# Mixer weights split once and loaded in parts by later blocks; layernorms' wide passes on VectorE

## The reference

```python
h = layernorm(concat([meta, x]), ln0_g, ln0_b)
proj = h @ w_in                       # q, k, v, conv B, C, h, and two gates
y_attn = window_attention(q, k, v, sinks) @ w_attn_out
y_conv = (cb * causal_conv3(cc * ch)) @ w_conv_out
mix = (sigmoid(ga) * y_attn + sigmoid(gc) * y_conv) @ w_o
h = layernorm(alpha * h + mix, ln1_g, ln1_b)
# then a router, top 2 of 32 experts, and a last layernorm
```

## Time and profile before

| | us |
|---|---|
| median of 3 runs | 4335.98 (4330.54 to 4336.49) |
| the profiled execution | 4333.28 |
| its span, first to last instruction | 4331.5 |
| first product of strip 0 in block 0, from the span's start | 62.7 |
| end of the last strip | 2690.2 |

### The profile page before, as it was taken

The page is one execution under the profiler, slowest core; times in us unless marked ns, Lnnn a source line. Parts: engine busy times, 40 slices in busy tenths (PEclk is TensorE's granted clock), DMA queues, the critical chain, the costliest instruction groups (busy, mean ns, idle before and its releaser), DMA issues. The chain is left out here.

```text
span 4331.5 us, 62892 instructions
## 1 busy us (share of the span) xinstructions
PE 4171.0 (96%) x20252; PEld 3428.8 (79%) x20253; DVE 2518.7 (58%) x3263; ACT 1773.0 (41%) x2950; POOL 1094.6 (25%) x1117
## 2 busy tenths in 40 slices
PE   7999999999999999999999999499999999999997
PEld 7887887887887888888888887388788888778886
DVE  5555555555555655645645645777666666765664
ACT  2422422422422422422422422466555555654553
POOL 4022032022022021121121121134333333333333
PEclk9999999999999999999999999799999999999998
DMA  6333333333333333333332332187666666765562
GB/s 171 85 107 103 93 102 98 99 104 97 102 104 89 107 106 85 107 104 89 111 102 80 117 102 78 54 289 248 246 199 198 206 199 234 251 203 198 194 204 90
DMA packets 569472, 601.49 MB, mean 139 GB/s; under 512 B 104080, under 2 KB 426640, under 8 KB 569248
## 3 DMA queue, kind: packets, MB, share of 16 engines
q1 hardware_dynamic: 521152, 476.88, 35.5%
q0 software_dynamic: 48096, 121.71, 8.4%
HBM read 527.15 MB, written 124.78 MB: 151 GB/s over the span
## 5 line engine op out<-in xcount | busy, mean ns | idle before, releaser
L826 PE MATMUL bank<-hT_hi,w_hi 128*128 128x512 f32 x2176 | 864.8, 397 | 30.1 <-DVE w_lo L658 21.3
L658 DVE TENSOR_TENSOR w_lo<-raw,w_hi 128x1024 fp32r<-128x1024 f32 x400 | 597.3, 1493 | 485.5 <-ACT w_hi L517 484.4
L827 PE MATMUL bank<-hT_lo,w_hi 128*128 128x512 f32 x2176 | 850.6, 391 | 2.4 <-issue 2.4
L828 PE MATMUL bank<-hT_hi,w_lo 128*128 128x512 f32 x2176 | 849.2, 390 | 0.0
L1565 PE MATMUL e_bank<-e_w_hi,e_xT_hi 128*128 128x512 f32 x1312 | 521.9, 398 | 14.2 <-DVE e_xT_lo L1488 12.4
L826 PEld LDWEIGHTS bank<-hT_hi,w_hi 128*128 128x128 f32 x2176 | 408.9, 188 | 140.4 <-DVE w_lo L658 32.6
L1567 PE MATMUL e_bank<-e_w_hi,e_xT_lo 128*128 128x512 f32 x1312 | 514.3, 392 | 0.0
L1566 PE MATMUL e_bank<-e_w_lo,e_xT_hi 128*128 128x512 f32 x1312 | 513.4, 391 | 0.0
L1493 DVE TENSOR_TENSOR e_w_lo<-e_raw,e_w_hi 128x1024 fp32r<-128x1024 f32 x384 | 444.4, 1219 | 117.7 <-ACT e_w_hi L1441 110.8
L828 PEld LDWEIGHTS bank<-hT_hi,w_lo 128*128 128x128 f32 x2176 | 408.9, 188 | 87.4
L827 PEld LDWEIGHTS bank<-hT_lo,w_hi 128*128 128x128 f32 x2176 | 409.3, 188 | 86.6 <-issue 5.4
(11 more groups left out here) (277 smaller groups left out, 7173.3 us busy)
## 6 DMA issues: line engine op xcount, KB each, us to landing
raw<-in_w_in_dram SPq DMA_DIRECT2D x251, 512.0 KB, 3.9
e_raw<-in_w_exp_gate_dram SPq DMA_DIRECT2D x128, 512.0 KB
e_raw<-in_w_exp_up_dram SPq DMA_DIRECT2D x128, 512.0 KB
e_raw<-in_w_exp_down_dram SPq DMA_DIRECT2D x128, 512.0 KB
h_rows<-h_rows SPq DMA_DIRECT2D x72, 512.0 KB, 3.5
raw<-in_w_o_dram SPq DMA_DIRECT2D x64, 512.0 KB, 3.8
raw<-in_w_in_dram SPq DMA_DIRECT2D x64, 256.0 KB, 3.7
raw<-in_w_attn_out_dram SPq DMA_DIRECT2D x64, 256.0 KB, 2.8
```

The source lines that it names most:

```text
L658: v.tensor_tensor(w_lo[:, s % 2, :], raw[:, s % RAW, :], w_hi[:, s % 2, :].bitcast(FP32), ALU.subtract).then_inc(lo_ready, 1)
L826: pe.matmul(out, hi, x_hi, start=first, stop=False)
L827: pe.matmul(out, hi, x_lo, start=False, stop=False)
L828: return pe.matmul(out, lo, x_hi, start=False, stop=last)
```

## The change

- In block 0 the weights are split as before, but two strips ahead, from 3 raw buffers, into three of four slots that each hold both parts of a strip; SP stores each split strip (1 MB) in DRAM, in `split_weights`.
- In blocks 1 to 7 no weights are split. SP loads both parts of strip s+3 from `split_weights` (1 MB, 8 KB per partition) into a slot, after strip s is done.
- The first block is written out ahead of a loop over the other seven.
- The layernorms of the loop do both wide passes on VectorE; GpSimd keeps the deviations.
- An `out` strip's first multiply waits for the last `mixT_lo`.

```diff
-    RAW = 5
+    RAW, META_RAW = 3, 5
+    SLOTS = 4
+    ahead = RAW
+    slot_of = list(range(SLOTS)) * 5 + [0, 1, 2] + list(range(SLOTS)) * 6 + [0, 1, 2]
+    def first_slot(s):
+        return (s + 1) % RAW
...
             def _(sp):
-                def load(s, b):
-                    hold(sp, lo_ready, b * N + s + 1)
-                    for dst, src in strip_dmas(*strips[s % N], raw[:, s % RAW, :]):
+                def load_raw(s):
+                    if s >= RAW:
+                        sp.wait_ge(lo_ready, s - RAW + 1)
+                    for dst, src in strip_dmas(*strips[s], raw[:, s % RAW, :]):
                         sp.dma_start(dst, src).then_inc(raw_in[s % RAW], 16)
-                load(0, 0)
-                with sp.Fori(0, BLOCKS) as b:
+                def store_split(s):
+                    sp.wait_ge(lo_ready, s + 1)
+                    sp.dma_start(split_d[s], slots[first_slot(s)][:, :, :].rearrange("p h d -> p (h d)").bitcast(FP32))\
+                      .then_inc(w_out[first_slot(s)], 16)
+                def load_split(s, b):
+                    sp.wait_ge(w_out[first_slot(s)], 16 * (sum(first_slot(q) == first_slot(s) for q in range(s + 1))))
+                    sp.dma_start(slots[slot_of[s]][:, :, :].rearrange("p h d -> p (h d)").bitcast(FP32), split_d[s])\
+                      .then_inc(w_in[slot_of[s]], 16)
+                def block_of_loads(b, first):
                     for s in range(N):
-                        load(s + 1, b)
+                        if first:
+                            store_split(s)
+                        if first and s + ahead < N:
+                            load_raw(s + ahead)
+                        else:
+                            hold(sp, strip_done, b * N + s + 3)
+                            if first:
+                                sp.wait_ge(w_out[first_slot(s)],
+                                           16 * (sum(first_slot(q) == first_slot(s) for q in range(s + 1))))
+                            load_split((s + ahead) % N, b + (s + ahead) // N)
                         if s - 3 in LN1_AT:
...
                         if s in X_AT:
...
@@ gpsimd
-                def scale(n, i1, rows, gain, shift):
-                    po.wait_ge(ln_normed, n + 1)
-                    po.tensor_tensor(rows[:, i1, :], rows[:, i1, :], gain[:, :], ALU.mult).then_inc(ln_scaled, 1)
-                    po.wait_ge(ln_scaled, n + 1)
-                    po.tensor_tensor(rows[:, i1, :], rows[:, i1, :], shift[:, :], ALU.add).then_inc(ln_done, 1)
...
@@ scalar, split_hi: in block 0 alone
+                        if first and s + 2 < N:
+                            split_hi(s + 2)
...
@@ vector
                 def normalize(n, i1, rows):
                     v.wait_ge(ln_moments, n + 1)
                     v.wait_ge(ln_rstd, 2 * n + 2)
-                    v.tensor_scalar(rows[:, i1, :], rows[:, i1, :], moments[:, i1, 0:1], rstd[:, i1, 0:1],
-                                    ALU.subtract, ALU.mult).then_inc(ln_normed, 1)
+                    gain, shift = (g1, b1) if rows is h else (g0, b0)
+                    v.scalar_tensor_tensor(out=rows[:, i1, :], in0=rows[:, i1, :], scalar=moments[:, i1, 0:1],
+                                           in1=gain[:, :], op0=ALU.subtract, op1=ALU.mult).then_inc(ln_normed, 1)
+                    v.wait_ge(ln_normed, n + 1)
+                    v.scalar_tensor_tensor(out=rows[:, i1, :], in0=rows[:, i1, :], scalar=rstd[:, i1, 0:1],
+                                           in1=shift[:, :], op0=ALU.mult, op1=ALU.add).then_inc(ln_done, 1)
...
-                        split_lo(s + 1)
+                        if first and s + 2 < N:
+                            split_lo(s + 2)
...
                             taken_by_act(s - 1)
                             got, taken, _ = output(s, 0)
+                            if i or not first:
+                                v.wait_ge(mlo_ready, b * KD + i)
...
@@ tensor
-                        pe.wait_ge(lo_ready, b * N + RAW + s + 1)
+                        if first:
+                            pe.wait_ge(lo_ready, s + 1)
+                            w_of = slots[first_slot(s)]
+                        else:
+                            pe.wait_ge(w_in[slot_of[s]], w_uses(s, b))
+                            w_of = slots[slot_of[s]]
...
+                block_of_strips(0, True)
+                with pe.Fori(1, BLOCKS) as b:
+                    block_of_strips(b, False)
```

More of the change, by code:

```diff
@@ L91, in mixer @@
     N = len(strips)
-    RAW = 5
-    assert N % RAW == 0 and N % 2 == 0
+    RAW, META_RAW = 3, 5
+    SLOTS = 4
+    ahead = RAW
+    slot_of = list(range(SLOTS)) * 5 + [0, 1, 2] + list(range(SLOTS)) * 6 + [0, 1, 2]
+    assert N == len(slot_of)
+    def first_slot(s):
+        return (s + 1) % RAW
     CONV0 = 2 + PAIRS
@@ L134, in sem @@
             return ctx.enter_context(nc.semaphore(name))
-        raw = sb("raw", [P, RAW, D])
-        w_hi = sb("w_hi", [P, 2, D], F32R)
-        w_lo = sb("w_lo", [P, 2, D], F32R)
+        split_d = nc.dram_tensor("split_weights", [N, P, 2 * D], FP32).ap()
         xs = sb("x_rows", [P, TILES, D])
@@ L173, in mixer @@
         arena = sb("arena", [P, 2 * KD * TOK])
+        weights = -(-nc.sbuf_base // 32) * 32
+        weight_space = sb("weight_space", [P, 9 * D])
         def place(at, name, shape, dt=FP32):
             size = 4 * math.prod(shape[1:])
-            assert at[0] + size <= shared + 4 * 2 * KD * TOK
+            assert at[0] + size <= (shared + 4 * 2 * KD * TOK if at[0] < weights else weights + 4 * 9 * D)
             placed = nc.alloc_sbuf_tensor_at(name, shape, dt, offset=at[0])
@@ L180, in place @@
             return placed
+        at = [weights]
+        slots = [place(at, f"w_slot{i}", [P, 2, D], F32R) for i in range(SLOTS)]
+        raw = place([weights + 4 * 6 * D], "raw", [P, RAW, D])
+        meta_raw = place([weights + 4 * 4 * D], "meta_raw", [P, META_RAW, D])
         at = [shared]
@@ L213, in mixer @@
             gains_in = sem1("gains_in")
-            raw_in = [sem1(f"meta_raw_in{i}") for i in range(RAW)]
+            raw_in = [sem1(f"meta_raw_in{i}") for i in range(META_RAW)]
             ln_step, ln_moments, ln_rstd, ln_gained, ln_done = (
@@ L237, in load_strip @@
                 def load_strip(n):
-                    for dst, src in strip_dmas(*meta_strips[n], raw[:, n % RAW, :]):
-                        sp.dma_start(dst, src).then_inc(raw_in[n % RAW], 16)
+                    for dst, src in strip_dmas(*meta_strips[n], meta_raw[:, n % META_RAW, :]):
+                        sp.dma_start(dst, src).then_inc(raw_in[n % META_RAW], 16)
                 sp.dma_start(hm, t["meta"]).then_inc(meta_in, 16)
@@ L245, in _ @@
                 sp.dma_start(xs[:, :, :], x[0:TOK, :].rearrange("(t p) d -> p t d", p=P)).then_inc(x_in, 16)
-                for n in range(1, RAW):
+                for n in range(1, META_RAW):
                     load_strip(n)
@@ L258, in _ @@
                     sp.dma_start(dst, row.unsqueeze(0).to_broadcast([P, row.shape[0]])).then_inc(consts_in, 16)
-                for n in range(RAW, len(meta_strips)):
-                    sp.wait_ge(pj_ready, n - RAW + 1)
+                for n in range(META_RAW, len(meta_strips)):
+                    sp.wait_ge(pj_ready, n - META_RAW + 1)
                     load_strip(n)
@@ L374, in _ @@
                 mm.then_inc(tp_ready, 1)
-                uses = [0] * RAW
+                uses = [0] * META_RAW
                 for what, n in order:
@@ L387, in _ @@
                     kind, i = meta_strips[n]
-                    uses[n % RAW] += 16 * len(strip_dmas(kind, i, raw[:, 0, :]))
-                    pe.wait_ge(raw_in[n % RAW], uses[n % RAW])
+                    uses[n % META_RAW] += 16 * len(strip_dmas(kind, i, meta_raw[:, 0, :]))
+                    pe.wait_ge(raw_in[n % META_RAW], uses[n % META_RAW])
                     if n == 0:
@@ L394, in _ @@
                     for k in range(KD):
-                        mm = pe.matmul(pj[n % 2][:, 0:META], raw[:, n % RAW, k * P:(k + 1) * P], hmT[:, k, :],
+                        mm = pe.matmul(pj[n % 2][:, 0:META], meta_raw[:, n % META_RAW, k * P:(k + 1) * P], hmT[:, k, :],
                                        start=(k == 0), stop=(k == KD - 1))
@@ L402, in mixer @@
         h1_out = [sem(f"h1_out{i}") for i in range(TILES)]
+        w_in = [sem(f"w_in{i}") for i in range(SLOTS)]
+        w_out = [sem(f"w_out{i}") for i in range(RAW)]
         hi_ready = sem("hi_ready")
@@ L439, in mixer, with raw_uses, w_uses @@
         LNS = 2 * TILES
[L441 to L446, removed]
+        def raw_uses(s):
+            return sum(16 * len(strip_dmas(*strips[q], raw[:, 0, :])) for q in range(s % RAW, s + 1, RAW))
+        def w_uses(s, b):
+            slot = slot_of[s]
+            return 16 * ((b - 1) * slot_of.count(slot) + slot_of[0:s + 1].count(slot))
         with nc.Block() as block:
@@ L473, in _ @@
```

(38 more changed lines are left out.)

12 lines of the change are left out of this document (3 added, 9 removed).

## The result

The changed kernel takes 4378.12 us (median of 4 runs, 4374.71 to 4389.7) against 4333.26 for the kernel before on the same chip: ratio 1.0108, 95% interval 1.0087 to 1.0129, 45 us slower. The forecast was 4390, range 4358 to 4420. The profiled execution took 4389.7 us; the forecast's sum for one was 4387.0.

What follows compares the result with a forecast made beforehand. The prediction took TensorE, busy 96% of the span, to bound the kernel. Its sum for a profiled execution was 4333.3 - 24.7 + 78.4 = 4387.0 us; with 2.7 us added for the median, 4390, range 4358 to 4420.

Steps and rivals of the forecast that it cites:

- What bounds: Mixer, first two thirds of the kernel: TensorE sets the pace, busy 96% of the span; only its waits count.
- Splits gone, 24.7 us: Mixer: TensorE's 20 waits for the low half of a weight strip go, a gain of 24.7 us.
- x moved behind strip 26, 9.2 us in seven blocks: Blocks 1 to 7, before strip 27: late `x` delays VectorE's multiply, so TensorE stalls 9.2 us per block.
- hand-over and SP's wake: End of strip 26: modelled overlap 0.17 us, then SP wakes in 0.2 us.
- to the issue of `x`: SP's queue after strip 26: the 1 MB load is issued, and `x` 0.8 us later.
- landing: `x` transfer before strip 27: arrives 5.6 us after its issue, queued behind 1 MB taking 2.6 us.
- measure: VectorE's iteration 26: ln0 statistics of the arrived `x` tile, 1.6 us.
- multiply and release: VectorE before strip 27: L767 empties strip 26's bank in 0.69 us, plus 0.15 to release TensorE.
- Clock, 2.0 us: After the stall in blocks 1 to 7: eight to ten products at half clock, 2.0 us lost per block.
- 1 MB loads hidden: Blocks 1 to 7: strip loads land after 4.7 us against a lead of 10.9 us, cost 0.
- Layernorm passes at no cost: Mixer layernorms: both wide passes on VectorE fit its free time, cost 0; 164 us if none were covered.
- The rivals: Before strip 27, no stall: 4311, chance 0.09; short stall: 4336, 0.03. At every strip, loads too slow: 4775, 0.04.

Runs made afterwards that it cites:

- `x` early: Changed kernel with the next block's `x` loads issued in SP's iterations 22 to 25 in place of 26 to 29: 4306.22 us, ratio 0.9935.
- the measure late: Changed kernel, `x` loaded as late as there, with VectorE's ln0 measures one strip later (27, 30, 33, 36): 4313.21 us, ratio 0.9941.
- one added wait in the kernel before: Kernel before, with SP holding tile 0's `x` load in iteration 26 until strip 26 is done: 4406.59 us, ratio 1.0171.
- doubled loads: Changed kernel with `x` early, plus a useless 1 MB DRAM copy ahead of each strip's 1 MB load: 4340.29 us, ratio 1.0007.

## Why the prediction was right, point by point

- *What bounds.* Right: VectorE lost 65 us per block and nothing came of it but the waits for `w_lo`.
- *Splits gone, 24.7 us.* With `x` early the last strip ends at 2664.9 in place of 2690.2, 25.3 us earlier, of which 0.8 lies ahead of the mixer's first product. Right in sum, but partly by luck. By the lengths of strips, 31 us went: the waits before strips 1, 5 and 7, and two things that I had not counted, the earlier kernel's pauses 13 products into a block (2.4 us of idle time) and 0.3 us before strip 14 in each block. Against that stand two new costs: the pause at the blocks' start (7.4 us) and a wait for block 1's strip 2, 1.7 us here and 1.9 in the changed kernel, where the granted clock then falls to 0.50 from 401.7 to 405.1. That wait comes from SP's list too: SP waits 7.6 us, until 396.34, for the store of strip 49 to land before it asks for block 1's strip 2.
- *x moved behind strip 26, 9.2 us in seven blocks.* Right in place, order and number, and shown three ways: it goes with `x` early, goes with the measure late, and comes with one added wait in the kernel before. The size was 8.72. Step by step, forecast and trace: hand-over and SP's wake 0.37 and 0.25, to the issue of `x` 0.8 and 0.74, landing 5.6 and 5.32, measure 1.6 and 1.61, multiply and release 0.84 and 0.75. Landing was mis-sized because I added the megabyte's 2.6 us whole; 2.1 of it shows. The packet records tell why: with nothing ahead of it, `x` moves its first packet 1.0 us after its issue; in the changed kernel the megabyte's packets go from 1259.03 to 1262.41 and `x`'s first at 1262.04, so that this 1.0 us passes while the megabyte moves.
- *Clock, 2.0 us.* 1.5 to 2.7 us per block, mean 2.2, from the length of strip 27. Together 7 x 10.9 = 76 against 78.4.
- *1 MB loads hidden.* Right for TensorE's waits: they land after 4.8 us (4.7 forecast), and doubled ones hold it up at 11 of 350 strips. Not foreseen was what they add at the blocks' starts. From 400 to 404, around the wait for block 1's strip 2, the trace has 430 GB/s. The Trainium skill, "DMA: Bandwidth & Descriptors", section Bandwidth, names about 358 GB/s as the limit that binds between HBM and SBUF, and the same section has 425 GB/s as measured for 16 MB with one core of the pair at work. The prediction gave the first figure alone; the trace agrees with the second:
```profile
400.00:404.00 4.00, 2.52 (x6) 1.95 (x7) 3.76 (x5) 0.17 (x1) 0.00 (x0) 0.72 1.02 430
```
- *Layernorm passes at no cost.* Right for this kernel. The reason I gave, that VectorE has no output to take in those iterations, was not enough: in the kernel before it had a split to make there, and only the change's other half took it away.
- *The rivals* fell: the pause is there, isn't short, and the loads keep pace.
- *What stays open.* The sum met the profiled execution (4387.0 and 4389.7), while the median of the runs is 12 us lower. The traces are of profiled executions only, so which term is smaller in the others stays open. The part behind the mixer, which the change leaves alone, takes from 1636.5 to 1649.1 us in the twelve profiled executions; a spread of that size lies outside the forecast's terms, so a match within 3 us is partly luck.

## What to carry to other kernels

When an in-order queue gets a new condition for one of its transfers, work out anew when every other transfer on it is issued, the untouched ones first: here a wait meant for weights moved the issue of a 512 KB activation load from 26 us ahead of its use to the moment when it was needed. Ahead of a wait that may be late, put everything that another engine needs. Price a part of a change with its neighbours: the same two passes cost 20 us beside the splits and nothing without them.

## What the runs showed of the hardware

At the start of blocks 2 to 7 TensorE paused for 0, 1.2 or 2.5 us, with no, one or two megabytes of loads under way. With 512 KB loads it paused there for at most 0.3 us, and a 16 KB instruction packet began 2.7 to 3.2 us before the block's first product in every case.

A pause of TensorE of 6 to 9 us put it at 0.50 of its clock each time, and about as many slow products followed one of 6.2 us as one of 8.7: strip 27 lost 1.5 to 2.9 and 1.5 to 2.7 us. Shorter pauses did it in some places and not in others: one of 1.9 us in the changed kernel did, those of 1.7 us in four of the experiments did not, and neither did one of 3.1 us with doubled loads.
